# An eighth weight slot in the residual's place, and Fox's output projection ahead of MLA's attention

## The reference

```
mix = concat([rmsnorm(o_fox, g_fox_out), rmsnorm(o_mla, g_mla_out)], axis=-1)
h = h + mix @ w_o
hid = silu(u @ w1[e]) * (u @ w3[e])
y = y + combine[:, e:e + 1] * (hid @ w2[e])
```

## Time and profile before

| | us |
|---|---|
| median of 3 runs | 628.41 (627.26 to 628.76) |
| the profiled execution, its own time | 628.14 |
| its span | 626.4 |
| TensorE busy | 587.5 (94%) |
| VectorE busy | 265.6 (42%) |
| ScalarE busy | 233.8 (37%) |
| GpSimd busy | 140.9 (22%) |
| moved by DMA | 141.64 MB, mean 226 GB/s |

### The profile page before, as it was taken

One profiled execution on the slowest core, in us unless ns is written; L12 is line 12 of the kernel. 1 busy time (PEld: TensorE's weight loads), 2 busy tenths in 40 slices (PEclk: granted clock), 3 DMA queues, 4 the chain that ended last, 5 costly groups with the idle time before them and its releaser, 6 DMA issues.

```text
span 626.4 us, 9256 instructions
## 1 busy us (share of the span) xinstructions
PE 587.5 (94%) x3559; PEld 408.1 (65%) x3559; DVE 265.6 (42%) x603; ACT 233.8 (37%) x445; POOL 140.9 (22%) x233
## 2 busy tenths in 40 slices
PE   8899999998999989999989999999999997877896
PEld 8778788786775447666778766566566554554554
DVE  3644245554484988437745771111111111101217
ACT  6826516543555473456616522212122121111220
POOL 6300001150233412122510011332322322212200
PEclk9999799999999989999989999999999999999999
DMA  8930000006400053000199499999999999999995
GB/s 274 335 121 1 0 2 0 1 2 239 182 1 0 34 235 135 10 1 1 30 427 413 146 412 370 372 397 379 395 393 384 389 398 393 394 395 391 398 378 216
DMA packets 32941, 141.64 MB, mean 226 GB/s; under 512 B 8689, under 2 KB 10785, under 8 KB 19841
## 3 DMA queue, kind: packets, MB, share of 16 engines
q1 hardware_dynamic: 26016, 127.02, 52.3%
q0 software_dynamic: 6304, 11.93, 5.8%
q10 hardware_dynamic: 576, 2.10, 0.8%
HBM read 132.85 MB, written 16.06 MB: 238 GB/s over the span
## 4 chain that ended last, share of the span: by engine, by line
PE 82%; DVE 10%; issue 4%; ACT 3%; POOL 1%; DVEq 0%; ACTq 0%; POOLq 0%
PE ps L2314 18%; PE ps L1953 16%; PE ps L2345 10%; PE ps L2149 6%; PE ps L2272 5%; PE ps L2032 4%; PE ps L2138 3%; PE ps L2087 3%; PE ps L2330 2%; PE ps L2107 2%; PE ps L1917 2%; DVE sums_s L1703 1%; PE ps L1926 1%; DVE x L1864 1%; PE ps L2193 1%
## 5 line engine op out<-in xcount | busy, mean ns | idle before, releaser
L2314 PE MATMUL ps<-w,xt 128*64 128x256 f32 x1024 | 116.6, 380 | 15.3 <-issue 15.0
L2314 PEld LDWEIGHTS ps<-w,xt 128*64 128x64 f32 x1024 | 76.9, 137 | 61.7 <-issue 33.0
L1633 DVE TENSOR_TENSOR xt<-ps,g_ffn_c 128x512 f32<-128x512 f32 x32 | 22.0, 692 | 187.1 <-PE ps L2272 187.1
L2345 PE MATMUL ps<-w,hT 128*64 128x512 f32 x256 | 61.8, 604 | 0.0
L1290 ACT ACTIVATE hsb<-ps,row_scale 128x256 f32<-128x256 f32 x32 | 15.2, 475 | 113.8 <-PE ps L2314 113.8
L917 POOL DMA_INDIRECT xg<-h_rows,idx x30 | 28.8, 960 | 109.0 <-PE ps L2272 108.6
L909 POOL DMA_INDIRECT y_rows<-yh,idy x29 | 29.5, 1016 | 65.3 <-ACT yh L1312 62.4
L2149 PE MATMUL ps<-probT,vals 128*128 128x512 f32 (+4 forms) x160 | 42.7, 411 | 1.0 <-POOL probT L846 1.0
L1714 DVE TENSOR_REDUCE nmax<-ps 128x1 bf16<-128x528 f32 (+1 forms) x64 | 28.0, 502 | 35.9 <-PE ps L2108 35.9
L846 POOL TENSOR_SCALAR_AFFINE_SELECT probT<-probT 128x128 f32<-128x128 f32 (+2 forms) x80 | 21.2, 288 | 83.8 <-ACT probT L1202 82.5
L2272 PEld LDWEIGHTS ps<-ident,xg 64*128 64x128 f32 x256 | 30.2, 200 | 11.6 <-issue 11.5
(11 more groups left out here) (353 smaller groups left out, 1061.8 us busy)
## 6 DMA issues: line engine op xcount, KB each, us to landing
w<-in_w SPq DMA_DIRECT2D x96, 1024.0 KB
x<-in_x SPq DMA_DIRECT2D x8, 512.0 KB, 9.5
y_rows<-zeros POOLq DMA_DIRECT2D x1, 4096.0 KB, 12.3
yg<-y_rows SPq DMA_DIRECT2D x4, 1024.0 KB, 11.0
w_in_v<-in_w_in SPq DMA_DIRECT2D x1, 2048.0 KB, 11.0
w_in_k<-in_w_in SPq DMA_DIRECT2D x1, 2048.0 KB, 16.8
w_in_q<-in_w_in SPq DMA_DIRECT2D x1, 2048.0 KB, 21.6
w_oa<-in_w_o SPq DMA_DIRECT2D x1, 2048.0 KB, 10.2
```

Source lines behind the costliest of these rows:

```text
L2314: ins = pe.matmul(ps[j * slots:(j + 1) * slots, 2 + b, 0:F], xt[b][:, k, :], w13[s][:, j, k, :], start=(k == 0), stop=(k == DK - 1))
L2345: ins = pe.matmul(ps[q * slots:(q + 1) * slots, 6 + b, :], hT[b][:, m, :], w2s[s][:, m, q * 512:(q + 1) * 512], start=(m == 0), stop=(m == ...
```

## The change

1. The place of x holds w1 and w3 of expert 7 as well, an eighth slot (`w13[RING]`, w2 in a place of its own). x is given up once h is stored to DRAM (`h_stored`), squared, and `first_tokens` is done, and is loaded again from h_rows by SyncE between w2 of expert 30 and w2 of expert 31. Slots are then found by `slot_of`, `loads_of`, `freed_by`: experts 8 and up use 7 slots in a ring.
2. The slots' places are exchanged. Experts 0 and 1, w1 of 6 and w2 of 7 are loaded once Fox's projection is complete, which is now before MLA's attention; experts 2 and 4 at its end; w2 of 5 after the last normalisation; the rest of 3, 5 and 6 after MLA's projection.
3. Fox's projection is made whole ahead of the first score of `attend(1)`: tile 0 and 1 in the last two turns of the up-projection, tile 2 behind them, tile 3 between the first two heads' max scores. The tiles lie in banks 4, 2, 0 and 0.
4. MLA's projection is divided by chunks of k. Chunks 0 and 1 of tile 0 are made after heads 14 and 15, then tile 1's, then chunk 2 of both, then chunk 3. From tile 2 on, `turn_u2`, `ranks` and `router` work two tiles behind the projection; four `keep_warm` calls go.
5. The high parts of Fox's w_o are made during Fox's attention, and three of four low parts too.
6. Small: one step less of semaphores in `first_slots`, `coef_diag` waits for one expert more.

```diff
-        slot_at = [r_qk, r_qk + SLOT, ring + SLOT, ring + 2 * SLOT, ring + 3 * SLOT, ring]
+        slot_at = [ring + SLOT, ring + 2 * SLOT, r_qk, ring + 3 * SLOT, r_qk + SLOT, ring]
...
+        w13.append(place(f"w13_{RING}", [P, 2, DK, F], F32, ring + HOLD * SLOT))
+        w2s.append(place(f"w2_{RING}", [P, FK, D], F32, r_last))
...
-        WEIGHT_AT = {H + 3: 4, H + 4: 6, GS - 2: 5, GS - 1: 7}
+        WEIGHT_AT = {3: 0, 4: 1, 5: 2, H - 1: 3, H + 3: 4, H + 4: 6, GS - 2: 5, GS - 1: 7}
+        LOW_AT = {4: (0,), 6: (1, 2), H + 4: (4,), H + 6: (6,), GS - 1: (5,)}
...
+            sp.wait_ge(wo_done, NT)
+            sp.wait_ge(y_zeroed, 16)
+            load_expert(0, 0)
+            load_expert(1, 1)
+            sp.dma_start(w13[6][:, 0, :, :], w1_v[6]).then_inc(w13_in[6], 16)
+            sp.dma_start(w2s[RING][:, :, :], w2_v[RING]).then_inc(w2_in[RING], 16)
             sp.wait_ge(scored, 3 * GS)
             sp.wait_ge(pv_done, GS)
...
             load_expert(2, 2)
+            load_expert(4, 4)
+            sp.wait_ge(o_done, DK)
+            sp.dma_start(w2s[5][:, :, :], w2_v[5]).then_inc(w2_in[5], 16)
             sp.wait_ge(wo_done, 2 * NT)
+            for s in (3, 5):
+                sp.dma_start(w13[s][:, 0, :, :], w1_v[s]).then_inc(w13_in[s], 16)
+                sp.dma_start(w13[s][:, 1, :, :], w3_v[s]).then_inc(w13_in[s], 16)
             sp.dma_start(w13[6][:, 1, :, :], w3_v[6]).then_inc(w13_in[6], 16)
             sp.wait_ge(logits_done, NT)
+            sp.dma_start(w2s[3][:, :, :], w2_v[3]).then_inc(w2_in[3], 16)
+            sp.wait_ge(first_done, 2)
+            sp.wait_ge(h_squares, NT)
+            for b in range(2):
+                sp.wait_ge(h_stored[b], 16 * NT // 2)
+            sp.dma_start(w13[RING][:, 0, :, :], w1_v[RING]).then_inc(w13_in[RING], 16)
+            sp.dma_start(w13[RING][:, 1, :, :], w3_v[RING]).then_inc(w13_in[RING], 16)
...
+            sp.wait_ge(tables_read, 1)
+            sp.dma_start(w2s[6][:, :, :], w2_v[6]).then_inc(w2_in[6], 16)
+            for e in range(FIRST, NE):
                 load_w13(e)
-                if e > RING:
+                if e > FIRST:
                     load_w2(e - 1)
...
+            for t in range(NT):
+                sp.dma_start(x[:, t, :], h_rows[t * P:(t + 1) * P, :]).then_inc(tile_in[t], 16)
             load_w2(NE - 1)
...
+                else:
+                    out_project(1, 0, 0)
+                    out_project(1, 0, 1)
                 turn_up(n)
-            out_project(1, 0, 0)
+            out_project(2, 0, 0)
+            out_project(2, 0, 1)
...
-            out_project(2, 0, 1)
-            out_project(3, 0, 0)
-            out_project(3, 0, 1)
-            sum_totals(1)
-            out_project(0, 1, 0)
-            out_project(0, 1, 1)
-            for p in range(1, NT):
+            for q in range(2):
+                out_project(1, 1, q, (0, 1))
+            for p in range(2):
+                for q in range(2):
+                    out_project(p, 1, q, (2,))
+            for p in range(2):
+                for q in range(2):
+                    out_project(p, 1, q, (HALF_K - 1,))
+                if p == 0:
+                    sum_totals(1)
+            for p in range(2, NT):
+                turn_u2(p - 2)
+                if p >= 3:
+                    ranks(p - 3)
                 out_project(p, 1, 0)
-                turn_u2(p - 1)
-                if p >= 2:
-                    ranks(p - 2)
-                keep_warm(WO_BANKS[p % 2] + 1, 4)
-                router(p - 1)
+                router(p - 2)
                 out_project(p, 1, 1)
```

More of the change, by code:

```diff
@@ L67 @@
 RING = 7
+FIRST = RING + 1
 HOLD = 4
@@ L271, in build @@
         HALF_K = DK // 2
-        wo_hi = [place(f"wo_hi{b}", [P, HALF_K, D], F32R, ring + SLOT * (1 - b)) for b in range(2)]
+        wo_hi = [place(f"wo_hi{b}", [P, HALF_K, D], F32R, ring + narrow * (1 - b)) for b in range(2)]
         wo_lo = [place("wo_lo0", [P, HALF_K, D], F32R, ring + 2 * SLOT),
@@ L467, in build @@
         hot_made, idx_done, idx_made = sem("hot_made"), sem("idx_done"), sem("idx_made")
-        w13_in = [sem(f"w13_in{s}") for s in range(RING)]
-        w2_in = [sem(f"w2_in{s}") for s in range(RING)]
+        w13_in = [sem(f"w13_in{s}") for s in range(FIRST)]
+        w2_in = [sem(f"w2_in{s}") for s in range(FIRST)]
         xg_in = [sem(f"xg_in{b}") for b in range(2)]
@@ L606, in unit_emptied, with first_slots @@
                 eng.wait_ge(unit_freed, sum(not of_act(u) for u in units[:n + 1]))
-        def first_slots(eng, p):
+        def first_slots(eng, step, p):
             i = TILE_ORDER[p]
@@ L642, in turn_bank, with slot_of, loads_of, freed_by @@
             return pair(4 + 2 * (n % 2), H * r)[0:FOX_AUG, :].rearrange("p (h c) -> p h c", h=H)
+        def slot_of(e):
+            return e if e < FIRST else (e - FIRST) % RING
+        def loads_of(e):
+            return 1 if e < FIRST else (e - FIRST) // RING + 2
+        def freed_by(e):
+            return e - FIRST if e < FIRST + RING else e - RING
         block = ctx.enter_context(nc.Block())
@@ L896, in _ @@
             for p in range(LAST):
-                first_slots(pool, p)
+                first_slots(pool, step, p)
             pool.wait_ge(idx_made, 1)
@@ L1729, in attend @@
                         normalise(g // 2 - 1, [g % 2])
-                    if g - 1 in WEIGHT_AT:
-                        weight_low(WEIGHT_AT[g - 1])
-                    if g in (GS - 2, GS - 1):
-                        mix_low(g - GS + 2 + HALF_K)
+                    for c in LOW_AT.get(g, ()):
+                        weight_low(c)
+                    if g == GS - 3:
+                        mix_low(HALF_K)
+                    if g == GS - 1:
+                        mix_low(HALF_K + 1)
             attend(0)
@@ L1774, in _ @@
             positions(LAST)
-            first_slots(dve, LAST)
+            first_slots(dve, step, LAST)
             dve.wait_ge(first_done, 2)
@@ L2005, in sum_totals, with out_project @@
                 ins.then_inc(sq_totals, 1)
-            def out_project(p, group, q):
+            def out_project(p, group, q, chunks=tuple(range(HALF_K))):
                 i = TILE_ORDER[p]
-                bank = WO_BANKS[p % 2]
-                pe.wait_ge(wo_hi_made, (group + 1) * HALF_K)
-                pe.wait_ge(mix_hi_made, (group + 1) * HALF_K)
-                pe.wait_ge(wo_lo_made, (group + 1) * HALF_K)
-                pe.wait_ge(mix_lo_made, (group + 1) * HALF_K)
+                bank = WO_BANKS[p % 2] if group else FOX_BANKS[p]
+                last = group * HALF_K + chunks[-1]
+                pe.wait_ge(wo_hi_made, max(WEIGHT_ORDER.index(group * HALF_K + c) for c in chunks) + 1)
+                pe.wait_ge(mix_hi_made, last + 1)
+                pe.wait_ge(wo_lo_made, max(WEIGHT_ORDER.index(group * HALF_K + c) for c in chunks) + 1)
+                pe.wait_ge(mix_lo_made, last + 1)
                 if group:
@@ L2022, in out_project @@
                         pe.wait_ge(mix_rooted, 1)
-                elif p == 1:
-                    pe.wait_ge(up_staged, NU)
-                elif p == 2:
-                    pe.wait_ge(maxed, NT * GS)
+                elif p < 3:
+                    pe.wait_ge(up_staged, NU - 2 + p)
                 else:
-                    pe.wait_ge(exped, 3 * GS)
+                    pe.wait_ge(fox_added, 3)
                 m_hi, m_lo, w_hi_o, w_lo_o = mix_hi[group], mix_lo[group], wo_hi[group], wo_lo[group]
                 for n, (m, w) in enumerate(((m_hi, w_hi_o), (m_lo, w_hi_o), (m_hi, w_lo_o))):
-                    for k in range(HALF_K):
+                    for k in chunks:
                         ins = pe.matmul(ps[:, bank + q, :], m[:, k, i * P:(i + 1) * P],
@@ L2034, in out_project @@
                                         stop=(n == 2 and k == HALF_K - 1))
-                if q == 1:
+                if q == 1 and chunks[-1] == HALF_K - 1:
                     ins.then_inc(wo_done, 1)
```

108 lines of the change are left out of this document (51 added, 57 removed).

## The result

The changed kernel took 635.00 us (median of 4 runs, 634.46 to 637.54) against 627.84 for the kernel before in the same session (4 runs, 626.17 to 628.76): a ratio of 1.0126, 95% interval 1.0099 to 1.0153. It is 7.2 us slower; the forecast said 627.0 in 621 to 632. The profiled execution took 634.46 for a span of 632.8, at a mean granted clock of 0.969 (before 0.988).

A forecast was written before the change was run, and what follows sets the result against it. The prediction took the expert weight stream to bound the kernel: last expansion 5.1 us earlier, tail 3.7 longer, together -1.4, a span of 625.0 and a predicted time of 627.0 us, range 621 to 632.

The forecast's parts named there:

- First score at 268.9: MLA's attention start: Fox's four tiles put ahead delay the first score by net 9.75 us, bounds 8 and 11.
- Attention's end near 320: End of MLA's attention, near 320 us; moved weight splits taken as 0, bounds -2 and +1.
- Chunk 3 idle for 3.3 and then at 1.2 GHz: After attention: TensorE waits 3.3 us for the last low part, then six matmuls take 2.7 us at 1.2 GHz.
- A routing round of 8.6: Routing after attention: ScalarE bounds each tile's round at some 8.6 us, instead of 9.74.
- Last projection at 351.2: The last output projection, which releases weight loads, stands at 351.2 us against 356.92 before.
- The first expert starts at 373.20 - 7.3 + 9.75 = 375.65: End of routing: 7.3 us saved after attention, 9.75 added before; first expert 2.4 later, bounds -2 and +5.
- rival C: Routing: TensorE falls to 1.2 GHz in new idle gaps, 5 us on the chain, total 632.0; chance 0.20.
- w2 of 6 at 382.3: Weight stream: expert 6's second weight waits for tables_read until 382.3 us, holding all later loads behind it.
- 3.00 us a load: Weight stream after restart: 71 loads at 3.00 us each, last expansion at 596.8, 5.1 us earlier than before.
- The tail: Last expansion to end: reloading x delays contraction and gathered rows, 28.2 us instead of 24.5, +3.7, bounds 2.5 and 5.5.
- B: Routing catches up: first expert starts 1 us earlier than before and the stream with it, total 623.7; chance 0.28.
- D: Stream: x's reload takes back the two early loads' gain, only restart cost 1.5 stays, total 629.9; chance 0.12.

The follow-up runs named there:

- e1: Changed kernel with more idle matmuls filling TensorE's gaps between the last routing steps; 2.6 us faster than the changed kernel.
- e3: Changed kernel with expert 8's first weights issued ahead of SyncE's wait for the tables and of expert 6's w2; median moved by 0.8 us alone.
- e5: Changed kernel with idle matmuls in the routing gaps and expert 8's first weights ahead of the tables wait; 629.87 us.
- e9: Changed kernel with routing gaps filled, expert 8's first weights early, residual reload behind the last weight, twelve idle matmuls in the wait at 327; 626.09 us.
- e11: Changed kernel with all three gaps filled and early first weights, but seven homes for expert weights and no residual reload; 628.83 us.
- e10: Kernel before with eight idle matmuls in its 1.68 us wait for the last sum of squares; 626.67 us.
- e2: Changed kernel with the residual's reload issued behind the last expert's second weight instead of ahead of it; 635.02 us.
- e7: Changed kernel with only the four idle matmuls ahead of each of the first three routers put back; 636.31 us.
- e12: Kernel before with only the residual's reload added ahead of the last second weight; medians 6.1 us apart, 5.1 us slower by the ratio.

## Why the prediction was wrong

The term that failed is the clock behind new waits of TensorE. The forecast let it fall at chunk 3 and took it as full everywhere else. By its steps, in order:

- First score at 268.9: it came at 269.30, 10.17 behind that of the kernel before where the working had 9.75. Right.
- Attention's end near 320: 320.96. The six matmuls put after head 15 waited 0.86 for a low part, which the forecast had at 0.
- Chunk 3 idle for 3.3 and then at 1.2 GHz: it was idle for 3.07, and the windows from 330 to 334 show 0.56 and 0.58. Right. The adds, though, began at 334.69 where the forecast had h of tile 0 done at 334.15.
- A routing round of 8.6: 8.72 and 8.56 on ScalarE. Right. Last projection at 351.2: 353.16.
- **"The first expert starts at 373.20 - 7.3 + 9.75 = 375.65": it started at 379.95. This is the step that failed.** It took the stretch from the last router to the first expert, 13.37 in the earlier trace rows, as unmoved; here it is 16.41 (379.95 - 363.54). e1 took 3.1 of the 4.3 back by filling gaps and nothing else, so they are the clock; the other 1.2 were there when attention ended (0.4 at the first score, the rest by the wait of 0.86). This is rival C, which had the place, the mechanism and the deciding point (over 3.5 later than 375.65) but a chance of only 0.20.
- "w2 of 6 at 382.3": 386.62, that is the same 4.3 later. The holes before 378 and around 386 are there as forecast; e3 and e5 show that the second one, made by SyncE's order, is worth some 2.5.
- 3.00 us a load and 214.5 from there to the last expansion: it was 216.53, so the forecast was 2.0 short. What makes it isn't settled: over 71 loads it would be 0.03 each, but the stream's mean rate from 390 to 600 us was 390 GB/s, against 389 in the kernel before, and the same term would hold a slower restart. Of the last ten experts only the last seven came 8.7 apart; the stream was not yet the limit before 542.
- **The tail, "+3.7, bounds 2.5 and 5.5": +5.17, inside the bounds.** The wait of the last contraction was forecast at 3.5 and measured 3.48. The 1.5 that is missing is that contraction at the lower clock behind the wait, 3.41 instead of 1.94: the same term that was left out in the routing, and not the rate of the loads. Where the clock did not fall, in e5, the tail was 28.1, against the 28.2 of the forecast. The working writes down only some of the pieces of its 28.2, so how well each was sized can't be told.

The sum of the errors: 4.3 + 2.0 + 1.5 = 7.8, which is 632.8 - 625.0. Of these, 3.1 and 1.5 are the clock. Rival C's 5 us for the routing was 1.9 more than the clock took there, and had nothing for the stream and the tail; that its 632.0 came within 3 us of the result is in part luck. B was wrong: the routing did not catch up, and even in e9, with every gap of the routing filled, the first expert stood at 374.71, later than the 373.20 of before. One of the arguments against B was misread, though to no effect: TensorE shows 8 and not 9 in slice 15 of the earlier trace rows. D was wrong too: e9 against e11 shows that the eighth home brings a net 2.7 us, 3 MB taken off the stream for 2 MB put back.

So the change is a gain of 2.7 (the eighth home), a loss of 2.2 by e11 against e10 (the order, gaps filled), and some 9 us, 635.0 against 626.1, that e9's four edits take back. Of these 2.6 are the routing's clock (e1), 2.5 the order of two loads (e5), and 3.8 what e9 adds to e5: the gap at 327, 1.5 by the first expert, and the reload's place, whose 0.8 of e2's tail doesn't make up the rest. That rest of 1.5 is left open. The profile of e5 can't settle it, since it is of the one run in which the last contraction was seen at full clock. If most runs of e5 lost up to 1.7 us there, as e1's profile did, that could make up the rest, for with the reload last nothing waits in front of this contraction; no trace shows it.

## What to carry to other kernels

When a change moves dense work (here projections) away from between short dependent steps, price the steps that stay behind at both clock levels, and do the same for every wait that a new transfer puts in front of products: here that was one and a half microseconds in a tail whose transfers were forecast well. Put idle matmuls where the new order has its gaps rather than where the old one had them. In a kernel whose end is set by a stream of weights, count bytes: what is loaded early is worth its bytes less those that it causes to be read again, and moving the reload behind another transfer mainly changed which engine was seen waiting. Compare an edit that fills gaps with the kernel before having its own gap filled; here 1.1 of the last 2.0 us were probably to be had there too. And before two profiles are compared, look whether each is of a middling run, and whether they differ already ahead of the edit.

## What the runs showed of the hardware

- The level of the clock in the same instructions differs from run to run. In the stretch from the third router to the first tokens the changed kernel fell twice and was back at 1.00 between; in e3 it stayed at 0.50 from 360 to 374, and the way from the first score to the first expert was 1.9 us longer (112.51 against 110.65).
- The same wait is followed by a fall in one run and not in another. Behind 3.43 to 3.48 us without work the last eight contraction matmuls took 3.41 in the changed kernel, 3.68, 3.18, 3.59 and 2.74 in e1, e3, e7 and e12, and 1.94 in e5, where every window of 2 us in that place shows 1.00.
- At the lower level sixteen router matmuls (128x36, fp32) took up to 3.60 us against 1.87, and four projection matmuls (128x512) 2.05 against 1.18: about the factor of two of the levels.
- The clock fell in the changed kernel behind a wait of 2.02 us, and in e7 behind one of 1.15 with four idle matmuls ahead of it. In e1, with these gaps filled, every window from 352 to 392 shows 1.00.
- A reload of 2 MB at the end of a full stream, estimated at 5.0 us from a window of 414 GB/s, made the tail 3.7 us longer at full clock (e5) and up to 5.6 where the clock fell behind the wait that it makes (e1); by the ratio of e12 it cost 5.1.
